# The mixing stage of a second transformer block in another order: convolution first, small products between weight units, and small banks evicted by two engines

## The reference, cut to what matters

```python
h = _rmsnorm(x, norm_mix[l])
z = h @ w_in[l]                       # 1024 -> 6936 columns
(q_n, kc, vc, ks, vs, kw, vw, g_n, q_r, k_r, v_r, g_r, c_a, c_b, m_g) = _split_cols(z)
o_nsa  = _nsa(...)          # 8 heads: compressed, selected and windowed attention, gated
o_ret  = _retention(q_r, k_r, v_r, g_r, ret_gn[l])        # rotary, 4 heads
o_conv = _conv_module(c_a, c_b, conv_w[l], conv_b[l], ...)  # causal, 31 taps, 512 channels
proj   = einsum('bsnc,ncd->bsnd', br, w_branch[l])        # three 512 -> 1024 products
merged = sum over the three branches of sigmoid(m_g) * proj
x = x + merged @ w_out[l]
h2 = _rmsnorm(x, norm_mlp[l])
x = x + square(relu(h2 @ w_ff1[l])) @ w_ff2[l]
```

## Time and profile before

| | us |
|---|---|
| median of 3 runs | 2710.39 (2708.49 to 2711.74) |
| the profiled execution, its own time | 2708.06 |
| its span | 2706.3 |
| PE busy | 2528.2 (93%) |
| PEld busy | 2070.4 (77%) |
| DVE busy | 2013.5 (74%) |
| ACT busy | 1446.5 (53%) |
| chain that ended last, share of PE / DVE / ACT | 81% / 15% / 2% |

### The profile page before, as it was taken

How to read it: one execution, slowest core, us unless ns; L and a number is a source line. 1 busy time by engine, 2 the same in 40 slices (tenths; PEclk the granted TensorE clock), 3 DMA queues, 4 the chain that set the end, 5 groups by cost and what they waited for, 6 DMA issues and landing times.

```text
span 2706.3 us, 30145 instructions
## 1 busy us (share of the span) xinstructions
PE 2528.2 (93%) x11758; PEld 2070.4 (77%) x11758; DVE 2013.5 (74%) x2558; ACT 1446.5 (53%) x1443; POOL 34.5 (1%) x46
## 2 busy tenths in 40 slices
PE   8799997999999999999999988898899998988998
PEld 6678876788888888888887877666678876666787
DVE  5665556889898989889898876597665556976655
ACT  4344442677777767677777654253444433534443
POOL 0000000000000000000000000000000000000000
PEclk9899998899999999999999998799999998999999
DMA  8255543699999999999999966233455552334553
GB/s 260 78 172 187 185 138 136 243 353 363 355 361 346 369 345 367 348 350 366 352 364 354 334 233 197 71 124 102 137 176 190 173 176 86 118 115 140 172 190 129
DMA packets 273709, 626.19 MB, mean 231 GB/s; under 512 B 17835, under 2 KB 27063, under 8 KB 273432
## 3 DMA queue, kind: packets, MB, share of 16 engines
q1 hardware_dynamic: 271404, 616.25, 65.6%
q0 software_dynamic: 1872, 6.82, 0.8%
q10 hardware_dynamic: 284, 1.12, 0.1%
HBM read 623.06 MB, written 1.07 MB: 231 GB/s over the span
## 4 chain that ended last, share of the span: by engine, by line
PE 81%; DVE 15%; ACT 2%; issue 1%; DMA 1%; POOL 0%; SPq 0%; POOLq 0%; DVEq 0%; ACTq 0%
PE tile L619 24%; PE tile L621 24%; PE tile L620 24%; PE aux L713 4%; DVE zbuf L2311 3%; DVE units_parts L1660 3%; PE aux L995 1%; ACT high L1273 1%; DVE units L1612 1%; PE aux L1108 1%; DVE sc L1833 1%; DVE x_sb L1716 0%; DVE acts L1619 0%; PE aux L1146 0%; DVE acc L1792 0%
## 5 line engine op out<-in xcount | busy, mean ns | idle before, releaser
L1660 DVE TENSOR_TENSOR units_parts<-units,high 128x1024 fp32r<-128x1024 f32 (+3 forms) x514 | 728.2, 1423 | 388.2 <-ACT high L1273 384.2
L1273 ACT ACTIVATE high<-units 128x1024 fp32r<-128x1024 f32 (+3 forms) x514 | 624.3, 1218 | 580.7 <-PE tile L621 536.8
L619 PE MATMUL tile<-high,acts 128*128 128x512 f32 (+2 forms) x1688 | 678.5, 402 | 27.2 <-DVE acts L1619 9.0
L620 PE MATMUL tile<-units_parts,acts 128*128 128x512 f32 (+2 forms) x1760 | 690.9, 393 | 0.0
L621 PE MATMUL tile<-high,acts 128*128 128x512 f32 (+2 forms) x1688 | 662.0, 392 | 0.0
L619 PEld LDWEIGHTS tile<-high,acts 128*128 128x128 f32 x1688 | 327.9, 194 | 113.8 <-DVE units_parts L1660 26.5
L620 PEld LDWEIGHTS tile<-units_parts,acts 128*128 128x128 f32 x1760 | 342.0, 194 | 63.7
L621 PEld LDWEIGHTS tile<-high,acts 128*128 128x128 f32 x1688 | 327.2, 194 | 67.2
L621 PE MATMUL tile<-high,zbuf_parts 128*128 128x512 f32 x692 | 270.9, 392 | 0.0
L620 PE MATMUL tile<-units_parts,zbuf_parts 128*128 128x512 f32 x632 | 245.9, 389 | 0.0
L619 PE MATMUL tile<-high,zbuf_parts 128*128 128x512 f32 x596 | 234.2, 393 | 0.0
(11 more groups left out here) (321 smaller groups left out, 3601.1 us busy)
## 6 DMA issues: line engine op xcount, KB each, us to landing
units<-in_moe_w SPq DMA_DIRECT2D x216, 1024.0 KB, 5.3
units<-in_w_in SPq DMA_DIRECT2D x136, 512.0 KB, 3.5
units<-in_w_ff SPq DMA_DIRECT2D x128, 512.0 KB, 3.6
q_buf<-in_moe_w SPq DMA_DIRECT2D x54, 1024.0 KB, 5.4
k_buf<-in_moe_w SPq DMA_DIRECT2D x54, 1024.0 KB, 5.3
nat<-in_moe_w SPq DMA_DIRECT2D x54, 1024.0 KB, 5.3
units<-in_ffn_w SPq DMA_DIRECT2D x62, 512.0 KB, 4.0
units<-in_w_out SPq DMA_DIRECT2D x32, 512.0 KB, 3.3
```

What stands on the lines that cost most here:

```text
L619: nc.tensor.matmul(bank, lhs[0], high, start=start, stop=False)
L620: nc.tensor.matmul(bank, lhs[0], low, start=False, stop=False)
L1273: nc.scalar.activation(high_slot(SG[0], n) if wide_ else high_slot(SG[0], n)[:, 0:cols], halves(weights) if wide_ else weights[:, 0:cols], ...
L1660: V.tensor_tensor(low, weights, high, ALU.subtract).then_inc(SG[0].low_ready, 1)
```

## The change

`ORDER2` puts tiles 6 and 7 (the convolution) first, then 1, 0, 2 and 3, and only two tiles are done before the small work starts (`EARLY2`). The taps, now counted one group of channels at a time (124 in all), lie at many more places: 28 between units, 16 around the compression, 8 before the compressed scores, 44 in the steps and 28 between the heads of retention. The compression has buffers of its own (`sc` and the place of `p_t`), so that it doesn't need the convolution's. The attention steps go through all heads of the first block of queries, then of the second, each with one unit; the unit stands last in a step, after scores, transposes and the values of the step before; rotary, its transposes, the first half of the attention's output and the gain of retention are set in at fixed steps. Scores are made negative (the queries are scaled by -`QSCALE`), so that DVE's eviction finds the minimum and ACT's exponential has scale -1: the separate negation is gone. The weights of two heads are computed at once (`weigh`). Each `aux` bank has a semaphore of its own, and ACT evicts the transposed queries, keys, compressed probabilities, rotary and convolution banks (`turn_in` on ACT, 16 banks a layer). Before `w_out`, the last branch product finishes the first block of tokens first (`tail=2`), and `w_out` starts on it (`wide_entered`). The first block's attention puts its unit last in a step too.

The diff, cut to its core:

```diff
-ORDER1, ORDER2 = [1, 2, 0, 3, 4], [0, 1, 2, 6, 7, 3, 4, 5] + list(range(8, 14))
-EARLY = 3
+ORDER1, ORDER2 = [1, 2, 0, 3, 4], [6, 7, 1, 0, 2, 3, 4, 5] + list(range(8, 14))
+EARLY, EARLY2 = 3, 2
-TURN2, STEPS2 = [1, 1, 1, 2, 3, 1, 1, 2, 1, 1], [1] * 16
-TAPS_TURN, TAPS_STEPS = [3, 2, 2], [1, 2] * 8
-AFTER2 = [4, 2, 0, 0, 0, 0]
+FILL2 = [1, 4, 2, 2, 1, 1, 1, 1, 1, 1, 1]
+ROTATE_AT, ROTATED_AT, NSA_AT, GAIN_AT = (2, 3), 6, 10, 13
+TAPS_FILL = [0, 12, 0, 6, 3, 2, 2, 3, 0, 0, 0]
+TAPS_CMP, TAPS_SCORES = (8, 8), 8
+TAPS_STEP = [2, 2, 0, 0, 2, 2, 2, 2] + [4] * 8
+TAPS_AFTER = [8, 8, 8, 4]
+AFTER2, BRANCH0, BRANCH1 = [1, 1, 1, 1], [1, 1, 2], [6, 2]
```

SP's queue, where the loads follow the new order, and the banks and wide products on TensorE:

```diff
-                    if i == len(ORDER2) - 4:
+                    if t == 5:
                         load_tables2(l)
...
             def aux_bank():
                 n = C.aux.take()
-                wait(pe, SG[0].aux_evac, n - 3)
+                if n >= 4:
+                    evacuated(n - 4)
                 return aux[n % 4]
+            def evacuated(n):
+                pe.wait_ge(SG[0].aux_evac[n % 4], n // 4 + 1)
...
-            def wide(units, lhs, between={}, when=None):
+            def wide(units, lhs, between={}, tail=0):
+                order = [(k, b) for k in range(units - tail) for b in range(TB)]
+                order += [(k, b) for b in range(TB) for k in range(units - tail, units)]
```

The small work on TensorE from the compressed probabilities on:

```diff
-                pipelined(NSA_H * TB, scores, turned, values, lambda u: go_on(later, STEPS2[u]))
+                scores(0)
+                scores(1)
+                pe.wait_ge(cmp_probs, l + 1)
+                turn_compressed(0)
                 go_on(later, next(fills))
+                values_compressed(0)
+                turn_compressed(1)
                 go_on(later, next(fills))
+                values_compressed(1)
+                for u in range(UNITS2):
+                    if u + 2 < UNITS2:
+                        scores(u + 2)
+                    turned(u)
+                    if u > 0:
+                        values(u - 1)
+                    if u == ROTATED_AT:
+                        pe.wait_ge(rot_ready, l + 1)
+                        turned_at["rot", l] = C.aux.n
+                        for b in range(TB):
+                            for h in range(2):
+                                turn([rot[:, b, 4 * h + i, :] for i in range(4)])
...
+                    if u == NSA_AT:
+                        turn_selected(0)
+                    go_on(later, 1)
+                values(UNITS2 - 1)
...
                 ret_scores(0)
                 for h in range(RET_H):
+                    go_on(later, next(fills))
                     if h + 1 < RET_H:
                         ret_scores(h + 1)
-                    go_on(later, next(fills))
                     ret_values(h)
+                    if h == 0:
+                        turn_selected(1)
                 aux_done()
                 wide(4, block_of(br_t[0]))
-                go_on(later, LEFT2 // 2)
+                go_on(later, next(fills))
+                pe.wait_ge(conv_out, 4 * (l + 1))
+                turned_at["y", l] = C.aux.n
+                for b in range(TB):
+                    turn([y_t[:, c, b * P:(b + 1) * P] for c in range(4)])
+                go_on(later, next(fills))
...
-                wide(4, block_of(br_t[2]))
-                turned_at[False, 5 + 4 * l + 2] = C.aux.n
-                turn_all(acc, 5 + 4 * l + 2)
-                wide(KC, lhs_act, when=arriving())
+                wide(4, block_of(br_t[2]), tail=2)
+                turn_block(acc, 0, stage)
+                wide_entered(acc, stage, turned_at[False, stage, 0], BLOCK0_UNITS)
```

New on ScalarE, the exponentials and the evictions:

```diff
+            def exps2(l, u):
+                nk, n = (u // NSA_H + 1) * P, scored_at["nsa", l, u]
+                act.wait_ge(S2.aux_evac[n % 4], n // 4 + 1)
+                for m in range(2):
+                    p = score_ring2[u % 4][:, m, 0:nk]
+                    e = nc.scalar.activation(p, p, ACT.Exp, scale=-1.0, bias=lowest2[:, u % 4, m:m + 1],
+                                             accum_out=dens2[:, u, m:m + 1])
+                e.then_inc(probs_ready, 1)
+            def turn_in(dst, n):
+                p, k, m = dst.shape
+                act.wait_ge(SG[0].aux_full, n + 1)
+                nc.scalar.activation(dst, aux[n % 4][0:64 if p == 64 else p, 0:k * m].rearrange("p (n m) -> p n m", n=k),
+                                     ACT.Copy).then_inc(SG[0].aux_evac[n % 4], 1)
```

VectorE's steps and its part of retention:

```diff
+                    if u in ROTATE_AT:
+                        rotate(ROTATE_AT.index(u))
+                    if u == NSA_AT:
+                        low_of([part[:, :, 0:P] for part in br_t[0]])
+                    if u == GAIN_AT:
+                        dve.wait_ge(tables_loaded, 16 * TABLES2 * (l + 1))
+                        evicted(5)
+                        for b in range(TB):
+                            V.tensor_tensor(z[:, 5, b, :], z[:, 5, b, :], ret_gn[:, :], ALU.mult)
+                    used(1, HIGHS - 2)
+                    taps_on(TAPS_STEP[u])
+                values(UNITS2 - 1)
...
+                for h in range(RET_H):
+                    used(AFTER2[h], HIGHS - 2)
+                    taps_on(TAPS_AFTER[h])
                     if h + 1 < RET_H:
                         ret_scores(h + 1)
                     ret_values(h)
+                    if h == 0:
+                        low_of([part[:, :, P:2 * P] for part in br_t[0]])
```

In the first block's attention, here on TensorE, a step's unit stands after its small products:

```diff
                 def between(u):
-                    go_on(later, STEPS1[u])
                     if l == 0 and u < NSA_H // 2:
                         flip_rows(1, u)
...
+                    go_on(later, STEPS1[u])
+                values(UNITS1 - 1)
                 turned_at[False, 3 * l, 0] = C.aux.n
                 turn_block(nat, 0, 3 * l)
-                values(UNITS1 - 1)
```

More of the change, by code:

```diff
@@ L1122, in _ @@
                 go_on(later, next(fills))
+                turn_queries(1)
+                go_on(later, next(fills))
                 aux_done()
@@ L1503, in _ @@
-                idle()
+                later.go_on(BRANCH0[2])
+                used(4)
+                later.go_on(1)
                 for b in range(TB):
@@ L2251, in _, with fill @@
+                tapped = []
+                def fill():
+                    units, taps_ = next(fills)
+                    for i in range(units):
+                        used(1)
+                        taps_on(taps_ // units)
+                fill()
                 for b in range(TB):
@@ L2371, in _ @@
[L2371 to L2380 removed]
+                    evac(V.scalar_tensor_tensor(o, bank[:, 64:128], coef2[:, u, 1:2], o, ALU.mult, ALU.add))
```

639 lines of the change are left out of this document (334 added, 305 removed).

## The result

The changed kernel takes 2594.81 us in the median of four runs (2592.38 to 2598.58), the kernel before 2709.44 beside it (2702.62 to 2711.74): a ratio of 0.9582, 95% interval 0.9561 to 0.9604. The forecast was 2629 with a range from 2600 to 2668.

A forecast was written before the change was run, and what follows sets the result against it. TensorE was taken to bound on average, with DVE full in the attention steps. Of 67.3 us lost a layer, 52.9 could be had; less 13 unseen, 40 a layer, 80 in two; first block -1: 2710.4 - 81 = 2629 us, range 2600 to 2668.

The forecast's parts named there:

- The first block: First block's attention: mixing ahead of other evictions cuts stalls, last heads' scaling comes later; -1 us in two layers.
- What I can't see: Second block's stage: in-order queues with hand-offs at some 40 new places cost 13 us a layer, between bounds 0 and 27.
- Compressed softmax and start of the steps: Second block, 1725 to 1753 us: units and key transposes hide the stalls; about 16 of 16.7 us saved a layer.
- The steps: Second block's attention steps: DVE falls to 69 us, below TensorE's 75.8; 10 of 11.7 us saved, 1.5 left for rotary steps.
- Retention: Retention's four heads: DVE with the added taps needs 20 us against TensorE's about 17; 3 us new a layer.
- Branches: Branch products: stalls go because DVE's retention work runs under the product, except perhaps 1.5 us a layer.
- The end: Stage's end before `w_out`: stall shrinks as the first tokens finish earlier; 4 us left a layer with the clock.
- Kept clock: Half clock after the compression and after the compressed scores stays in both kernels: about 4 us a layer.
- all hand-offs fit: Rival: nothing of the 13 us unseen hand-off cost appears, 26 us more gained, 2603 us; chance 0.14.
- The steps gain nothing: Rival: DVE and TensorE both near 76 us in the steps, which stay as before; 13 a layer, 2655 us; chance 0.16.
- ACT is late: Rival: evictions on ACT stand behind high parts, exponentials or table loads; 17.5 us a layer, 2664 us; chance 0.10.
- The clock falls: Rival: TensorE's lower clock level holds through the steps, which take twice 76 us; +76 a layer, 2781 us; chance 0.04.

The follow-up runs named there:

- e1: Changed kernel with the whole first-block part (order of its steps, and its end) put back as before: 2608.6 us, ratio 0.9641.
- e2: Changed kernel with only the order inside the first block's eight steps put back, the new end kept: 2616.4 us, ratio 0.9662.
- e13: Changed kernel with two neighbours swapped at the first block's end, low parts made before the next weight unit's split: 2586.4 us, ratio 0.9555.
- e9: Changed kernel with weight units taken out from between the small products before the second block's steps, most put ahead of the compression: 2619.1 us, ratio 0.9675.
- e5: Changed kernel with the old order inside the second block's 16 attention steps: 2598.3 us, ratio 0.9592.
- e6: Changed kernel with the 16 small banks a layer that ACT evicts evicted by DVE instead: 2600.3 us, ratio 0.9612.
- e10: Changed kernel with 96 of the convolution's taps in the attention steps, 6 in each, none in compression, compressed scores or retention: 2611.3 us, ratio 0.9652.
- e7: Changed kernel with the 28 taps between retention's heads moved into the attention steps, 4 or 5 a step: 2601.5 us, ratio 0.9604.
- e16: Changed kernel with 12 of retention's 28 taps moved into six of the first eight steps, run beside e15 on one chip: 2590.2 us, ratio 0.9564.
- e8: Changed kernel with the end of the second block's mixing stage as before on TensorE: 2600.3 us, ratio 0.9599.
- e11: Changed kernel with DVE evicting the first block's extra banks at the end of the step again, not behind the next mixing: 2609.0 us, ratio 0.9635.
- e4: Changed kernel with DVE splitting weight units three ahead again, not two, in the first block's steps: 2599.0 us, ratio 0.9606.
- e15: The changed kernel itself, unedited, run again beside e16 on one chip: 2595.2 us, ratio 0.9587.
- e12: Changed kernel with the first block's old end and 12 of retention's taps moved into the second block's first steps: 2580.4 us, ratio 0.9524.
- e14: Changed kernel with 12 of retention's taps moved into the first steps, the same kernel as e16 in another group: 2593.6 us, ratio 0.9583.

## Why the prediction was wrong in size

**The first block, "I take -1" (bounds -8 and +4): measured -15.6 in the profile, -14 by e1.** This is the first failed step. I had the mechanism, the wait of the earlier trace rows cut by mixing ahead of the other evictions, and sized it by that row alone. Three things were left out. One is the second name of the same wait, which stands beside it in the same list of the kernel before:

```profile
PE aux L713 <- DVE sc L1994: 5.8, 4, 2.8
```

Another is the clock behind a stall, though I had stated for the second block that a stall costs itself and 1.5 to 2.5 us more. The third is the second layer, where the two names wait 5.2 and 5.4 us. Together 23.8 us of such stalls stood in the kernel before and 4.7 stand in the changed one, and the wait on `x_sb` in the second layer fell with them (12.6 to 8.2); e2 measures 22 for the steps. Against it stands a loss that I did expect to be possible and put in the wrong place: I feared the late scaling of the last heads; e13 shows 8 us from the split set ahead of the low parts.

**"What I can't see", 13 us a layer: measured 3 or less.** This is the second failed step. The layer's loss fell by 49.7 us (77.5 to 27.8) where 40 was forecast. The terms that I had named as left over, 16.5 us, are 15.3 by the rows after (below), so by the difference to the 52.9 us that could be had the unseen hand-offs cost 3 to 4. The rows leave even less for them: behind the entry, from 1632 to 1887 us, the six stretches lose 9.1 us idle and 6.6 of clock, and nearly all of it has one of the names below. I had taken their price from the stalls of the old steps and "two of the large ones' clock": the price of hand-offs without cover. e9 shows that this price is real, 12 to 13 us a layer, once the units between are gone; e5 shows that with a unit between an eviction and its reader the order doesn't matter, and e6 that this is nearly so even with all evictions on DVE, as long as DVE has time to spare (the kernel before and e10 had the unit too, and waited). The count of hand-offs (40 new places) was not the number to look at; whether each has a unit in front of it was, and whether DVE's sum leaves room, and code and sums told that.

**Compressed softmax and start of the steps, 16 of 16.7 saved: right.** No idle time from 1662 to 1788 us. **The steps, 10 saved: a little low.** Forecast in 78 us, they take 76; DVE's sum, forecast at 69, is 66. The rotary steps, for which I left 1.5, show no wait; with four groups of taps in each and more around them, in e7, 3.6 us of waits follow. **Retention, 3: right**; the four heads take 18.6 us (forecast 20), and a wait of 2.8 stands behind them, ahead of the first branch product; e16 gives 2.5 a layer back. **Branches, 1.5: too low**, 2.3 and 1.1 us of waits on the first two branch products' evictions. **The end, 4: too high**, 1.7 ahead of `w_out` and 1.0 inside it; e8 prices the whole edit at 2.8 a layer. **Kept clock, 4: right**, 0.15 x 23 + 0.06 x 27 = 5.1. **First fills, 2.5: too high**, 1.3. **ACT's evictions at nothing: right**, no wait on ACT, which is busy 136 of 276 us and evicts in 0.58 us:

```profile
L1436 ACT ACTIVATE q_buf<-aux 64x512 f32<-64x512 f32 x8 | 4.2, 584 | 1.9 <-PE aux L735 1.9
```

**Loads at nothing: right.** TensorE waits for no load, and SP's queue waits mostly for units as in the earlier trace rows:

```profile
SPq L467 <- PE tile L630: 248.3, 71, 12.7
```

Of the rivals, "all hand-offs fit" (2603) was the nearest and right in its mechanism; it was given 0.14, and the reason against it, "any bunching shows", was too strong by e5 and e6, while e7 has a bunch that does show, 3.6 us in the steps. "The steps gain nothing" fell with DVE at 66 of 76; e10 shows what it takes to make it true, 52 more groups of taps. "ACT is late" has no row (the range, said to take in half of this case, took in all of it: 2664 lies under 2668). "The clock falls" did not happen in the steps (1.00) and happened in e9. The low end of 2600 is the perfect fit (2603) with a first block of -1 in it: the two failed terms pointed the same way, and the range let neither move with the other.

What stays open: e11 accounts for 14 of the steps' 22 us; the unit's place in the step, with a small part at most for the distance of the split (e4), should be the rest, but it was not run alone.

## What to carry to other kernels

Price a hand-off by what lies between its producer and its reader on the waiting engine, and by the room that the producing engine has: with one unit of 2.8 us in front, and DVE at 66 of 76 us, it cost nothing here in either order, and 2.7 us a layer with all evictions on DVE; with the unit and DVE full (the kernel before, e10) it waited; and with the units taken from the chain before the steps it cost 12 us a layer, most of it as a lower clock and not as idle time. When a wait's price is read from a list, add up all names under which the same line appears, add the clock behind it, and multiply by the layers. And look at what a reordering puts ahead of the operation that the busiest engine wants next: two lines swapped at one place were worth 8 us of a change of 115.

## What was not expected of the hardware

TensorE busy 25 of 26 us ran at a granted clock of 0.71 in e9, with 45- and 15-column products, transposes and less than three units among them; in the steps, 76 of 76 us busy with a unit in each, at 1.00. So the share of busy time alone does not tell which of the two levels (1.2 and 2.4 GHz) is granted.

From the compression's first product to the first attention scores the same code takes 33.8 us in the changed kernel's profile, 32.1 in e15's and 36.8 in e12's, by the moment at which the half clock after the compression ends. The changed kernel:

```profile
1673.70:1677.70 4.00, 4.00 (x14) 3.38 (x15) 1.70 (x5) 0.95 (x3) 0.00 (x0) 0.54 0.00 0
1677.70:1685.70 8.00, 8.00 (x62) 7.41 (x61) 5.12 (x12) 5.40 (x9) 0.00 (x0) 1.00 0.54 156
```

and e12, which has the same code there:

```profile
1660.80:1664.80 4.00, 4.00 (x14) 3.43 (x14) 1.44 (x5) 0.88 (x2) 0.00 (x0) 0.50 0.00 0
1664.80:1672.80 8.00, 8.00 (x51) 7.04 (x50) 4.04 (x9) 3.96 (x6) 0.00 (x0) 0.82 0.46 130
```

That, several times in a run, may be much of the spread of 3 to 12 us among five runs of one kernel (no run took it apart), and it may be why e14 showed nothing sure where e16 beside e15 showed 5 us.
